# An overflow block of a mixture of experts that takes its weights from a slot already filled

## The reference, cut to what matters

```
g_sel = argmax(t @ w_rg + b_rg)                      # one of 4 groups
top_p, top_i = top_k(softmax(e_logits[g_sel]), 2)    # 2 of its 8 experts
expert_id = g_sel * 8 + top_i                        # 1024 (token, expert) pairs, 32 experts
hid = silu(xb @ w_gate[e]) * (xb @ w_up[e])          # 1024 -> 256, per expert
y   = hid @ w_down[e]                                # 256 -> 1024
x  += sum over a token's two experts of gate * y
```

## Time and profile before

| what | value |
| --- | --- |
| median of three executions | 2454.94 us |
| profiled execution, its own time | 2454.77 us |
| its span in the trace | 2452.9 us |
| PE, busy share of the span | 93% |
| DVE, ACT, POOL | 41%, 24%, 16% |
| queue q1, share of 16 DMA engines | 42.2% |
| the two expert stages, by the first and last gate-and-up | 458 to 693 us and 1217 to 1454 us |

### The profile page before, as it was taken

The page is one execution under the profiler, slowest core; times in us unless marked ns, Lnnn a source line. Parts: engine busy times, 40 slices in busy tenths (PEclk is TensorE's granted clock), DMA queues, the critical chain, the costliest instruction groups (busy, mean ns, idle before and its releaser), DMA issues. The chain is left out here.

```text
span 2452.9 us, 29166 instructions
## 1 busy us (share of the span) xinstructions
PE 2282.5 (93%) x11800; PEld 1693.5 (69%) x11800; DVE 995.8 (41%) x1711; ACT 587.6 (24%) x1213; POOL 401.8 (16%) x399
## 2 busy tenths in 40 slices
PE   7989999898889989999899888899999999999998
PEld 6667788554447767788654446787767887888887
DVE  5545533411145444643421116344653334332234
ACT  2533401311123342410311114323441002100012
POOL 2011121121111101111122111111101121121111
PEclk9999999899999999999899999899999999999999
DMA  5114536799962202233899982332212332333321
GB/s 160 48 50 107 134 104 257 311 422 422 422 243 68 69 27 71 67 97 145 323 416 421 423 350 93 94 92 67 83 55 78 105 110 86 94 95 95 102 96 69
DMA packets 291897, 402.86 MB, mean 164 GB/s; under 512 B 31534, under 2 KB 230958, under 8 KB 273834
## 3 DMA queue, kind: packets, MB, share of 16 engines
q1 hardware_dynamic: 276000, 372.56, 42.2%
q0 software_dynamic: 10176, 16.81, 1.8%
q10 hardware_dynamic: 5578, 11.51, 1.8%
HBM read 388.98 MB, written 30.15 MB: 171 GB/s over the span
## 5 line engine op out<-in xcount | busy, mean ns | idle before, releaser
L138 PE MATMUL banks<-h_split,w_high 128*128 128x512 f32 x2624 | 827.7, 397 | 2.3 <-PEq L3240 1.7
L138 PEld LDWEIGHTS banks<-h_split,w_high 128*128 128x128 f32 x2624 | 482.0, 189 | 104.0 <-issue 8.2
L190 DVE TENSOR_TENSOR w_low<-w_raw,w_high 128x1024 fp32r<-128x1024 f32 (+1 forms) x264 | 316.7, 1201 | 503.9 <-POOL w_high L179 503.9
L179 POOL CAST w_high<-w_raw 128x1024 fp32r<-128x1024 f32 (+1 forms) x264 | 276.5, 1048 | 1461.6 <-PE banks L138 1337.3
L138 PE MATMUL banks<-h_split,w_low 128*128 128x512 f32 x1312 | 513.1, 391 | 0.0
L138 PEld LDWEIGHTS banks<-h_split,w_low 128*128 128x128 f32 x1312 | 246.8, 188 | 52.8
L138 PE MATMUL banks<-w_high,op_split 128*128 128x512 f32 x736 | 228.5, 390 | 1.4 <-DVE mg_part L1355 1.1
L2012 PE MATMUL banks<-expert_ring,ex_xsT 128*64 128x256 f32 x1472 | 184.1, 407 | 32.8 <-DMA expert_ring<-in_w_exp_up 32.8
L2012 PEld LDWEIGHTS banks<-expert_ring,ex_xsT 128*64 128x64 f32 x1472 | 108.7, 146 | 95.2 <-DMA expert_ring<-in_w_exp_up 36.2
L138 PEld LDWEIGHTS banks<-w_high,op_split 128*128 128x128 f32 x736 | 138.2, 188 | 31.7 <-DVE mg_part L1355 2.4
L138 PE MATMUL banks<-w_low,op_split 128*128 128x512 f32 x368 | 143.4, 390 | 0.0
(11 more groups left out here) (423 smaller groups left out, 2698.2 us busy)
## 6 DMA issues: line engine op xcount, KB each, us to landing
w_raw<-in_w_in SPq DMA_DIRECT2D x142, 512.0 KB, 3.9
expert_ring<-in_w_exp_gate SPq DMA_DIRECT2D x46, 1024.0 KB, 20.2
expert_ring<-in_w_exp_up SPq DMA_DIRECT2D x46, 1024.0 KB, 23.4
expert_ring<-in_w_exp_down SPq DMA_DIRECT2D x46, 1024.0 KB, 23.2
w_raw<-in_w_gu SPq DMA_DIRECT2D x44, 512.0 KB, 3.8
region<-in_w_exp_gate SPq DMA_DIRECT2D x20, 1024.0 KB, 20.7
region<-in_w_exp_up SPq DMA_DIRECT2D x20, 1024.0 KB, 23.6
region<-in_w_exp_down SPq DMA_DIRECT2D x20, 1024.0 KB, 23.5
```

The source lines that it names most:

```text
L138: last = nc.tensor.matmul(out, left, right, start=(start and n == 0), stop=(stop and n == 2), skip_group_check=True)
L179: self.nc.gpsimd.tensor_copy(self.high[:, i % self.SPLIT, 0:n], self.raw[:, i % self.RAW, 0:n]).then_inc(self.high_ready, 1)
L190: self.nc.vector.tensor_tensor(self.low[:, i % self.SPLIT, 0:n], self.raw[:, i % self.RAW, 0:n], self.high[:, i % self.SPLIT, 0:n].bitcast ...
```

## The change: the first overflowing expert and expert 26 change places

Let E be the first expert with more than 64 tokens. Block E gets the tokens and the weights of expert 26, and block 26 those of expert E. The loads of blocks 6 to 31 read their expert number from a row `order` that VectorE writes. The overflow block no longer has a load; it is worked at position 30, ahead of the blocks 30 and 31, from the slot of block 26 (slot 2), which is not loaded again. If E is below 6, whose weights are loaded before the routing is known, no places are changed, and GpSimd refills slot 2 with expert E by four indirect DMAs (`refill`). These four are issued in every execution; where nothing is to be refilled all their indices lie beyond the bounds. TensorE waits for all four before position 30. SP's wait ahead of the four pieces of the next matrix goes from `e.blocks - 2` to `e.blocks - 1`.

```diff
+            sp.wait_ge(order_ready, 1)
+            pair = [(n, e.expert(sp, n)) for n in (EXPERT_SLOTS, EXPERT_SLOTS + 1)]
             for part in (e.load_gate_up, e.load_down):
-                for n in (EXPERT_SLOTS, EXPERT_SLOTS + 1):
-                    part(sp, n, n)
+                for n, expert in pair:
+                    part(sp, n, expert)
             for n in range(EXPERT_SLOTS + 2, EXPERTS):
-                e.load(sp, n)
-            sp.wait_ge(spill_ready, 1)
-            for n in range(EXPERTS, e.blocks):
                 e.load(sp, n)
...
-            sp.wait_ge(e.down_done, e.blocks - 2)
+            sp.wait_ge(e.down_done, e.blocks - 1)
...
+            def first_ending(out, weight, total):
+                link(V.scalar_tensor_tensor(out=out, in0=ends[:, 1:], scalar=0.5, in1=weight, op0=ALU.is_gt, op1=ALU.mult))
+                link(V.scalar_tensor_tensor(out=out, in0=ends[:, 0:NE], scalar=0.5, in1=out, op0=ALU.is_lt, op1=ALU.mult,
+                                            accum_out=total))
+            V.scalar_tensor_tensor(out=delta[:], in0=ends[:, 0:NE], scalar=float(LANES), in1=spill_base[:], op0=ALU.mult,
+                                   op1=ALU.add)
+            first_ending(moved[:], step[:], moved_sum[:])
+            link(V.scalar_tensor_tensor(out=moved[:], in0=home[:], scalar=moved_sum[:], in1=moved[:], op0=ALU.mult,
+                                        op1=ALU.subtract))
+            link(V.tensor_tensor(delta[:], delta[:], moved[:], ALU.add),
+                 V.tensor_tensor(slotv[:], slotv[:], tiled(moved[:], NE), ALU.subtract))
...
+            V.tensor_tensor(moved[:], base[:, 0:NE], moved[:], ALU.subtract).then_inc(link_sem, 1)
             e.weigh(dve, 0)
+            V.tensor_scalar(r.order[:], moved[0:1, :], 1.0 / LANES, None, ALU.mult).then_inc(order_ready, 1)
...
+RESIDENT = 26
+ORDER = (*range(EXPERTS - 2), EXPERTS, EXPERTS - 2, EXPERTS - 1)
...
+    def refill(self, pool, last_row):
+        gu, down = self.slots[RESIDENT % len(self.slots)]
+        w_gate, w_up, w_down = self.weights
+        rows = "l e (p c) n -> (l e p) (c n)"
+        pool.wait_ge(self.gu_done, RESIDENT + 1)
+        pool.wait_ge(self.down_done, RESIDENT + 1)
+        for out, weights, column, last in ((gu[:, 0, :], w_gate.rearrange(rows, c=DC), 0, last_row[0]),
+                                           (gu[:, 1, :], w_up.rearrange(rows, c=DC), 0, last_row[0]),
+                                           (down[:, 0, :], w_down.rearrange("l e r n -> (l e r) n"), 1, last_row[1]),
+                                           (down[:, 1, :], w_down.rearrange("l e r n -> (l e r) n"), 2, last_row[1])):
+            self.nc.gpsimd.indirect_dma_start(out=out, out_offset=None, in_=weights,
+                                              in_offset=bass.IndirectOffsetOnAxis(ap=self.r.refill[:, column:column + 1], axis=0),
+                                              bounds_check=last, oob_is_err=False).then_inc(self.refilled, 16)
...
+            if refill_ready and n == RESIDENT + 2:
+                pool.wait_ge(refill_ready, 1)
+                self.refill(pool, last_weight_row)
             self.scatter(pool, n, last_row)
...
-        gu = self.slots[n % U][0].rearrange("p g (c n) -> p g c n", c=DC)
-        pe.wait_ge(self.w_landed[n % U], 32 * (n // U + 1))
+        gu = self.slots[held % U][0].rearrange("p g (c n) -> p g c n", c=DC)
+        pe.wait_ge(self.w_landed[held % U], 32 * (held // U + 1))
+        if self.refilled and self.order[n] == EXPERTS:
+            pe.wait_ge(self.refilled, 16 * 4)
```

More of the change, by code:

```diff
@@ L1453, in __init__ @@
         self.gate = sb("gate", [P, 2, NT])
-        self.token = sb("token", [P, BLOCKS // 2], I32)
+        self.token = sb("token", [P, BLOCKS // 2 + 1], I32)
+        self.order = sb("order", [1, EXPERTS], I32)
+        self.refill = sb("refill", [P, 3], I32)
         self.row = sb("row", [P, BLOCKS], I32)
@@ L1519, in merge_and_route @@
         spill_f = sb("spill_f", [P, SPILL + 1])
+        step, home, moved, back = (sb(n, [P, NE]) for n in ("step", "home", "moved", "back"))
+        moved_sum, refill_f = sb("moved_sum", [P, 1]), sb("refill_f", [P, 4])
         (landed,) = first.landed
@@ L1834, in _ @@
             lanes_hot(slice(4, 8))
+            V.tensor_tensor(moved[:], base[:, 0:NE], moved[:], ALU.subtract).then_inc(link_sem, 1)
+            done[0] += 1
             e.weigh(dve, 0)
+            dve.wait_ge(link_sem, done[0])
+            V.tensor_scalar(r.order[:], moved[0:1, :], 1.0 / LANES, None, ALU.mult).then_inc(order_ready, 1)
             dve.wait_ge(tabled, 1)
-            for half, lanes in enumerate((slice(0, LANES), slice(LANES, P))):
-                V.tensor_scalar(r.token[lanes, :], k.ps[lanes, 7, half:BLOCKS:2], 2.0 * S, None, ALU.add).then_inc(token_ready, 1)
+            halves = tuple(enumerate((slice(0, LANES), slice(LANES, P))))
+            last_pairs = ((15, 16, (EXPERTS, EXPERTS - 2)), (16, 17, (EXPERTS - 1, EXPERTS + 1)))
+            for half, lanes in halves:
+                V.tensor_scalar(r.token[lanes, 0:15], k.ps[lanes, 7, half:EXPERTS - 2:2], 2.0 * S, None, ALU.add)\
+                    .then_inc(token_ready, 1)
+            for half, lanes in halves:
+                for start_at, stop_at, blocks in last_pairs:
+                    V.tensor_scalar(r.token[lanes, start_at:stop_at], k.ps[lanes, 7, blocks[half]:blocks[half] + 1], 2.0 * S, None,
+                                    ALU.add)
+                V.tensor_scalar(r.token[lanes, 17:], k.ps[lanes, 7, EXPERTS + half:BLOCKS:2], 2.0 * S, None, ALU.add)
             dve.wait_ge(gexp_done, NT)
@@ L1859, in _ @@
                  V.tensor_copy(spill_f[:, SPILL:SPILL + 1], ends[:, NE:]))
-            V.tensor_copy(r.spill_expert[:], spill_f[0:1, :]).then_inc(spill_ready, 1)
+            V.tensor_copy(r.spill_expert[:], spill_f[0:1, :])
+            first_ending(back[:], back[:], refill_f[:, 0:1])
+            link(V.scalar_tensor_tensor(out=refill_f[:, 1:2], in0=refill_f[:, 0:1], scalar=float(P), in1=values[:, 0:1],
+                                        op0=ALU.mult, op1=ALU.add),
+                 V.scalar_tensor_tensor(out=refill_f[:, 2:3], in0=refill_f[:, 0:1], scalar=float(HID), in1=values[:, 0:1],
+                                        op0=ALU.mult, op1=ALU.add))
+            V.tensor_scalar(r.refill[:, 0:1], refill_f[:, 1:2], 2.0 * S + NOWHERE * P, None, ALU.add)
+            V.tensor_scalar(r.refill[:, 1:2], refill_f[:, 2:3], 2.0 * S + NOWHERE * HID, None, ALU.add)
+            V.tensor_scalar(r.refill[:, 2:3], refill_f[:, 2:3], 2.0 * S + NOWHERE * HID + P, None, ALU.add).then_inc(refill_ready, 1)
             e.vectors(dve, 2)
@@ L1920, with __init__ @@
 class Experts:
-    def __init__(self, k, ctx, tag, tiles, r, layer, first, blocks, xn_rows, y_rows, weights, slots, found):
+    def __init__(self, k, ctx, tag, tiles, r, layer, order, tokens_at, xn_rows, y_rows, weights, slots, found):
         self.k, self.nc, self.r, self.layer, self.weights = k, k.nc, r, layer, weights
-        self.first, self.blocks, self.pairs = first, blocks, -(-blocks // 2)
-        assert first % 2 == 0
+        self.order, self.tokens_at = order, tokens_at
+        self.blocks, self.pairs = len(order), -(-len(order) // 2)
+        self.refilled = None
         self.xs, self.xsT, self.silu_out, self.hid, self.hidT, self.y = tiles
@@ L1937, in expert, with held @@
     def expert(self, sp, n):
-        b = self.first + n
-        return b if b < EXPERTS else sp.value_load(self.r.spill_expert[0:1, b - EXPERTS:b - EXPERTS + 1], min_val=0,
-                                                   max_val=EXPERTS - 1)
+        order, at = (self.r.order, n) if self.refilled else (self.r.spill_expert, n)
+        return sp.value_load(order[0:1, at:at + 1], min_val=0, max_val=EXPERTS - 1)
+    def held(self, n):
+        if not self.refilled:
+            return n
+        return self.order[n] if self.order[n] < EXPERTS else RESIDENT
+    def refill(self, pool, last_row):
[11 more added lines that the diff above has]
+                                              bounds_check=last, oob_is_err=False).then_inc(self.refilled, 16)
     def load_gate_up(self, sp, n, expert):
@@ L1963, in gather @@
     def gather(self, pool, q, last_token, token=None):
-        at = self.first // 2 + q
+        at = self.tokens_at + q
         token = self.r.token[:, at:at + 1] if token is None else token
@@ L1976, in scatter @@
         pool.wait_ge(self.y_ready, n + 1)
-        at = self.first + n
+        at = self.order[n]
         self.nc.gpsimd.indirect_dma_start(out=self.y_halves, in_=self.y[:, n % OUTPUTS, :], in_offset=None,
@@ L2032, in down @@
                                              self.hidT[:, n % 2, LANES * f:LANES * (f + 1)],
-                                             self.slots[n % U][1][:, f, h * 512:(h + 1) * 512], start=(f == 0), stop=(f == 1))
```

(7 more changed lines are left out.)

26 lines of the change are left out of this document (15 added, 11 removed).

## The result

The changed kernel takes 2462.3 us (median of 7 runs, 2459.2 to 2469.1), against 2454.4 us for the kernel before on the same chip (7 runs): a ratio of 1.0042 with a 95% interval of 1.0028 to 1.0056, or about 10 us [6.9 to 13.7] more. The forecast was slower, 2468.7 us, with 2457.5 to 2480 as its range: the sign and the place were right, the forecast's size, +13.8 us, lies just above that interval. The medians are 7.9 us apart. The profiled execution of the changed kernel is the lowest of its runs, 2459.18 us with a span of 2457.4, only 4.5 us above the span before.

The account below looks back on a forecast made before the run. TensorE is busy 93% of the span, but weight loads limit the end of each expert stage. Load saved, refill wait and slow clock sum to +13.8 us on 2454.77: 2468.6, median 2468.7 us, range 2457.5 to 2480.

Parts of the forecast that it names:

- The load that goes: End of both expert stages: without block 32's load position 32 starts 5.8 and 5.9 us earlier; with layer 1's clock, 13.4 us.
- last 80 us: End of layer 0's expert stage: DMA share full at about 421 GB/s, so the weights are the limit there.
- The wait that comes: Before position 30: TensorE stands for the four empty refills, whose packets take turns with the weights' packets; 10.9 us in layer 0.
- Behind it 36 x 0.28 = 10.1 us: Refills on q0: 36 packets per engine at 0.28 us each, counted from the landing of position 27's scatter.
- The clock: Position 30's gate and up: half the granted clock after the wait adds 2.9 us a layer, bounds 1.7 and 4.
- The edits at nothing: Longer routing chain, expert numbers read by SP, later pieces of the next matrix: all hidden, 0 us.
- A: Before position 30: refills without data land some 2 us after issue, nearly in time; gain 11.4 us, 2443.5 us; chance 10%.
- B: Before position 30: each refill lands 7.6 us after its own issue, side by side; +5.9 us, 2460.8 us; chance 14%.
- C: Refills: an expert below 6 overflows, so they move 3 MB and the load isn't saved; 2476 us; chance 2%.
- D: Loads of 26 blocks: SP falls behind by 1 us each wherever the queue runs empty; beyond 2480 us; chance 3%.

## Why the prediction was right, and where its size was off

*The load that goes: right.* Forecast 13.4 us; without the refills the kernel gains 11.3 us [8.1 to 14.5], and by the traces 5.0 + 4.9 + 1.7 = 11.6 (good to 1 or 2 us a layer, as said above). The "last 80 us" of full DMA share in the forecast rest on a row of 40 us; from 610 to 690 us the share is 1.00 at 414 GB/s, so the reading holds.

*The wait that comes: right in kind, too long.* 36 packets per engine, no bytes, one packet for a row: as forecast. The forecast put the last refill's landing 17.2 and 16.5 us behind the scatter's start; in the run position 30 starts 14.25 and 14.35 us behind it. The term "Behind it 36 x 0.28 = 10.1 us" failed in where it starts and in the price of a packet. The refills needn't wait for the scatter to land: by its landing, at 670.75, 95 of their packets had been served. Queue q0 is served from 668.6 us, 4.1 us after the scatter's start (14 or 15 packets went before that), and the last refill lands 10.0 us later, at 678.6: 5 + 36 packets per engine, 0.24 us each on the mean. But this mean isn't a turn. From 670 to 674 us:

```profile
q1 hardware_dynamic: 258, 1.40, 83.5%
q0 software_dynamic: 357, 0.05, 7.7%
```

That is 16 packets of q1 and 22 of q0 for each engine in 4 us, 0.18 us for one of q0: what a packet more cost between 20 and 36. From 674 to 678 us q0 has only 249 (0.26 us each) beside 216 of q1; why it slows down isn't shown. I had taken the middle between 0.24 and 0.33 us. The 0.33 of the earlier trace rows has a slow start and a tail in it: from 1416 to 1418 us of the same trace q0 has 142 packets, 0.23 us each. And the 0.24 of the earlier trace rows took for granted that the queues alternate one for one, packets as the profile counts them. The rule of the Trainium skill (DMA: Bandwidth & Descriptors, section Queues, rings and completion order) is turns of a whole packet, typically 9 to 17 descriptors. The trace agrees in that both queues move on side by side; one for one the profile's packets don't alternate, 357 to 258 here and 520 to 397 in layer 1 from 1434 to 1440 us, and no run shows how they relate to the rule's packets.

The wait of 9.33 and 7.93 us (forecast: 10.9 and 10.4) is the distance less the time in which TensorE is still busy: 4.9 and 6.4 us between the scatter's start and the end of the turning, 6.3 and 6.0 in the kernel before. In the change and the three versions with fewer packets this last lies between 4.9 and 6.4 us.

*The clock: right in kind, too high.* Position 30 took 1.8 us longer than at full clock, not 2.9: the 5.36 us of the earlier trace rows were the nearer row, though the wait is longer than for either.

| term, both layers | forecast | shown |
| --- | --- | --- |
| the load that goes, with layer 1's clock | -13.4 | -11.6 |
| the wait | +21.3 | +17.3 |
| half clock at position 30 | +5.8 | +3.6 |
| sum | +13.7 | +9.3 |

(The forecast's +13.8 is the same sum rounded at other places; the stages' own balance after is +8.9, the ratio +10.3 [6.9 to 13.7], the medians +7.9. The first row of "shown" comes from the version without refills, the other two from the change.)

*The edits at nothing: right.* The routing's part is in this trace of the changed kernel (start, length):

```profile
446.88 0.19 DVE L1826 SCALAR_TENSOR_TENSOR rt_delta<-rt_ends,rt_spill_base 128x32 f32<-128x32 f32 x1
448.15 0.29 DVE L1833 SCALAR_TENSOR_TENSOR rt_over<-banks,rt_delta 128x128 f32<-128x128 f32 x1
...
453.54 1.88 PE L1657 MATMUL banks<-rt_block_token,rt_lane_hot 128*128 128x48 f32 x8
```

From the first to the second it is 1.27 us, 0.22 before: 1.05 us more, inside the forecast's 1.0 to 1.3. Position 0's gate and up follows at 455.35, right behind the last row's matmuls. In layer 1 position 0 starts 528.9 us after layer 0's position 32, 528.2 before and 526.0 to 528.8 in the other versions. That this delays nothing that can be measured is shown by the version with these edits alone, 0.9999. SP takes 1.14 us from the start of one expert's last load to that of the next expert's first, where it took 0.43, and the DMA share stays full.

The next matrix's first piece came in time, cast 9.9 us after position 32's start, as forecast; the third was waited for, 0.43 us, inside the forecast's bound of 1.

*The rivals.* A (in time, 2443.5) would show no wait; there is one of 9.33 us. The Trainium skill's 2.0 us plus bytes (same page, section Anatomy of one DMA — SWDGE (gpsimd) path) holds here for a scatter on idle queues, 2.0 us, and not for a refill of no bytes beside the weights, which took 6.6 to 9.0 us. B (only the latency, each by itself: 6.6 us of wait) gave 2460.8, nearer to the median of 2462.3 than my own 2468.7, and the time alone can't reject it: its +5.9 lies 1 us below the interval of 6.9 to 13.7, my +13.8 just above it. The trace does: the last refill is issued at 669.70 and TensorE starts 9.0 us later, not 7.6; and B has no room for the 3 us between refills of 128 and of 64 rows, nor for last refills that land 5.2 to 8.9 us after their start. That the number came out inside the range is in part luck: the wait and the clock were put 6.2 us too high and the gain 1.8 too high, which cancel in part. C falls by q0's unchanged 16.81 MB, D by the steady window.

## What to carry to other kernels

Before taking a load away, ask what the work it allowed to come earlier will now stand behind: here 3 MB less a layer were worth 5 to 6 us, and four DMAs that moved nothing cost 10 us a layer, since they were waited for. A conditional DMA isn't free where its condition is false: count its rows as packets, here some 0.2 us for each that a DMA engine has to pass beside the busy queue. Put such DMAs where no one waits for them (with the block last they cost nothing), or leave the rare case to a path that exists anyway; and put a block that needs no load before the last loads, not behind them, so that they can run ahead (0.9946 at position 28, 0.9979 at the last). No input was run in which an expert below 6 overflows; there the refills would move data, and the versions without them would pay for the second stage.

## What the runs showed of the hardware

An indirect DMA with all rows out of bounds still sends its packets: 9 per DMA engine for 128 rows, 5 for 64 and 3 for 32, for rows of 8 KB as for the gather's. On idle queues 80 such packets went in 0.2 us, 5 for each engine; beside the weights 22 for each engine took 4 us, 0.18 us each. Of an engine's time such a packet took 0.014 us there and a packet of the weights 0.21 us (7.7% and 83.5% of 16 engines' 4 us), so most of the price is the other queue's packets.

Beside the weights q0's packets began to flow 4.1 us after the start of position 27's scatter, and 95 packets of the refills behind it were served before it had landed.

In the idle time from 669.37 to 678.70 us the granted clock was 1.00 until 672 us, then fell to 0.50, the level of 1.2 GHz, stayed there until 682 us, in the middle of position 30's gate and up, and was 1.00 again from 683 us. A gate and up took 5.52 us after that wait and 5.46 after 7.93 us, and 5.70, 6.29 and 6.13 us after waits of 5.72, 5.37 and 5.85 us. The longer wait didn't cost more of the clock.
